# Writing out TensorE's loops over heads and head pairs in a two-layer streaming encoder step

## The chip, the cores and the metric

One Trainium2 chip, one core of it. The time is device microseconds of one execution of the program. Three executions of the kernel before took 3556.9, 3558.29 and 3559.72 us; the median, 3558.29 us, is the time before.

## The reference, cut to what matters

Two consecutive encoder layers are evaluated in one step for a prompt of 1024 frames and a sample of 32 frames, all in float32. Model width is 1024.

```python
# layer 0: x += W_out[ concat( A * silu(zA), B * silu(zB) ) ]
#   A: gated delta rule, 8 heads of 128, causal conv of width 4 on q, k, v,
#      blocks of 64 frames with a triangular solve, state (8, 128, 128)
#   B: chunk-band softmax attention, 16 heads of 64, own chunk and the 8 before it,
#      QK-RMSNorm, learned bias by clipped distance
# layer 1: x += W_out[ GLA * silu(z) ], gated linear attention, 8 heads,
#      dk = 128, dv = 256, gate from a rank-16 projection, state (8, 128, 256)
# after each layer: x += 4-head cross-attention into 256 memory tokens, gated
...
def gdn_block(S, q, k, v, g, beta):
    ...
    sol = lax.linalg.triangular_solve(a_mat, rhs, left_side=True, lower=True)
    u = sol[..., :A_DV] - jnp.einsum('bhjd,bhdv->bhjv', sol[..., A_DV:], S)
    qk = jnp.einsum('bihd,bjhd->bhij', q, k) * dec
    o = (jnp.einsum('bihd,bhdv->bhiv', q, S) * jnp.exp(G)[..., None]
         + jnp.einsum('bhij,bhjv->bhiv', qk, u))
...
def _softmax_attend(q, k, v, bias, valid):
    s = jnp.einsum('bqhd,bkhd->bhqk', q, k).astype(jnp.float32) * (q.shape[-1] ** -0.5)
    ...
    p = jax.nn.softmax(s, axis=-1).astype(v.dtype)
    return jnp.einsum('bhqk,bkhd->bqhd', p, v)
...
def gla_block(S, q, k, v, lg):
    ...
    o = (jnp.einsum('bihd,bhdv->bihv', q * jnp.exp(cb), S)
         + jnp.einsum('bhij,bhjv->bihv', att, v))
```

## The kernel before, in words

The kernel is a row of stages, each a block of five hand-written instruction streams (TensorE, ScalarE, VectorE, GpSimd and the DMA-issuing SyncE) that meet only in counting semaphores; a barrier of all engines stands between two stages (line 45). The stages are: `turn_input` (transposes the input), `gdn` (the delta rule, with the input projection of its heads), `band` (band attention), `finish_layer` for layer 0, `gla` (linear attention) and `finish_layer` for layer 1.

Within `gdn`, `band` and `gla` the work goes head by head. `gdn` and `gla` have 8 heads each; `band` has 8 pairs of heads, since a pair of heads of 64 fills the 128 partitions. On TensorE a head's or a pair's own small matmuls are interleaved by hand with the large projection matmuls of the next one: `fill(n)` lets n steps of the generator `project`, `stream`, `mem_steps` or `early_steps` through, so the order of TensorE's instructions is fixed when the program is built. In `band` the generator `stream(n + 1, 1 - p)` gives the next pair's projection (lines 1462, 1470, 1477 to 1485, 1492), while `scores(u)` (lines 1520 to 1526), `turn(u)` (line 1536) and `values(u)` (line 1556) belong to the pair at hand. `gdn` projects at line 510, `gla` at lines 2020 and 2024.

The first head and the last are written out, since their waits or their filling differ. The heads between them are a loop that the engine's own sequencer runs:

```python
with pe.Fori(1, H_A - 1) as h:      # gdn, line 720: 6 passes, one head each
    head(h, True, True)
...
with pe.Fori(0, 3) as i:            # band, line 1580: 3 passes, two pairs each
    pair(i * 2 + 1, 1, True)
    pair(i * 2 + 2, 0, True)
...
with pe.Fori(1, H_C - 1) as h:      # gla, line 2135: 6 passes, one head each
    head(h, True)
```

In `band` a pass holds two pairs because buffers alternate by the parity of the pair. Tile addresses in a pass are constants; what depends on the pass is the value that each wait compares a semaphore with, such as `h * 6 + 2`, which is computed in registers. A loop's end is a compare and a branch back to its first instruction. The other engines have loops of their own over the same heads (lines 451, 911, 1117 and 1234 in `gdn`, 1427, 1680, 1803 and 1825 in `band`, 1977, 2236, 2348 and 2386 in `gla`).

At the start of a pair in `band`, SyncE issues the load of the next pair's fourth weight tile (line 1366), the stores of the pair's values (lines 1398 and 1399), the store of the attention output (line 1407) and the load of cached values (line 1372). ScalarE copies projections out of PSUM, computes the gate (line 1630, between two loads of activation tables) and the exponentials (line 1648); VectorE adds bias and takes the maximum (lines 1723 and 1726) and normalises (line 1744).

Of the kernel before, what the change touches and what calls it, by code (L numbers as in the profile page):

```python
# [201 lines left out]
H_A = 8  # L202
# [14 lines left out]
def gdn(nc, ident, ones, eps, hT, W, w_ld, w_in, conv_w, conv_state, a_log, dt_bias, onorm_g, state_in,  # L217
# [4 lines left out]
    with ExitStack() as ctx:  # L222
# [65 lines left out]
        mT = [[BT, VV], [KR, KE]]  # L288

        w_mkv = [w.rearrange("(k p) n -> p k n", p=128) for w, _, _, _ in mem_layers]  # L290
        W_mem = [W[:, 2 * x:2 * x + 2, :, :].rearrange("p j k n -> p (j k n)").rearrange("p (k n) -> p k n", k=4) for x in (1, 0)]
        mem_tiles = [[tap[:, 0:1024], U[:, 2, 0:1024]], [zraw[:, 0:1024], sall[:, :, :].rearrange("p h n -> p (h n)")[:, 0:1024]]]
# [77 lines left out]
        with nc.Block() as block:  # L370
# [129 lines left out]
            def _(pe):  # L500
# [216 lines left out]
                pe.wait_ge(padded, 1)  # L717
                pe.wait_ge(o_padded, 1)
                head(0, True, False)
                with pe.Fori(1, H_A - 1) as h:  # L720
                    head(h, True, True)
                head(H_A - 1, False, True)
                turn_out(H_A - 1, 2)
# [534 lines left out]
def band(nc, ident, ones, eps, hT, W, w_ld, w_in, q_g, k_g, rel_bias, cache_k, cache_v, bias_rows,  # L1258
# [6 lines left out]
    with ExitStack() as ctx:  # L1265
# [96 lines left out]
        with nc.Block() as block:  # L1362
# [87 lines left out]
            def _(pe):  # L1450
# [126 lines left out]
                    if m + 1 == ends[place["k", 0]]:  # L1577
                        pe.wait_ge(consts, 2)
                pair(0, 0, True)
                with pe.Fori(0, 3) as i:  # L1580
                    pair(i * 2 + 1, 1, True)
                    pair(i * 2 + 2, 0, True)
                pair(7, 1, False)
# [247 lines left out]
H_C, DV_C, RANK, TAU = 8, 256, 16, 16.0  # L1831
# [14 lines left out]
def gla(nc, ident, ones, eps, hT, W, w_ld, w_in, w_up, gate_bias, onorm_g, state_in, o_dram, state_p, state_s,  # L1846
# [6 lines left out]
    with ExitStack() as ctx:  # L1853
# [76 lines left out]
        SLOT, FIRST = GLA_SLOT, GLA_FIRST  # L1930
        STRIDE = {"q": 128, "k": 128, "z0": 256, "z1": 256}
        LAST = {kind: max(m for m, (x, _) in enumerate(PLAN) if x == kind) for kind in ("z0", "z1", "v", "q", "k")}
        LAST0 = {kind: max(m for m, (x, _) in enumerate(PLAN0) if x == kind) for kind in ("z0", "v", "z1", "q", "k")}


# [23 lines left out]
        with nc.Block() as block:  # L1959
# [46 lines left out]
            def _(pe):  # L2006
# [125 lines left out]
                    if i + 1 == KD * Z0_END:  # L2132
                        turn_lr()
                head(0, True)
                with pe.Fori(1, H_C - 1) as h:
                    head(h, True)
                head(H_C - 1, False)

# [1063 lines left out]
```

## Time and profile before

| what | value |
|---|---|
| median of three executions | 3558.29 us (3556.9 to 3559.72) |
| the profiled execution's own time | 3559.13 us |
| its span, first to last instruction | 3557.4 us |
| TensorE busy in the span | 3482.5 us (98%) |
| VectorE, ScalarE, GpSimd busy | 1173.9, 1102.7, 512.3 us |
| mean granted TensorE clock | 0.994 |
| instruction pages fetched by DMA | q8: 99 packets, 1.62 MB; q14: 62 packets, 0.51 MB |

The profile takes one execution; its span lies 1.7 us under that execution's own time, and that time 0.84 us over the median. PE is TensorE's matmul side and PEld its weight loads, which overlap it; PEldq is TensorE's sequencer, likewise DVEq and ACTq for VectorE and ScalarE. A TensorE wait whose releaser reads "issue" is time in which the engine waited for no semaphore that the profile shows.

### The profile page before, as it was taken

How to read it: one execution, taken by the hardware profiler on the slowest of the kernel's cores; microseconds unless marked ns; L12 is line 12 of the kernel's file. 1: busy time of each engine (PE TensorE's matmuls, PEld its weight loads, DVE VectorE, ACT ScalarE, POOL GpSimd, SP SyncE). 2: the span in 40 equal slices, each digit the busy share in tenths (PEclk: the TensorE clock that was granted, in tenths of full speed). 3: DMA queues.
4: the chain of work that ended last, by engine and by line, in shares of the span. 5: the costliest groups of instructions: out<-in, count | busy, mean ns of one | idle time of the engine just before them, and what ended most of it. 6: DMA issues, size and time to landing. Idle time of an engine off the chain costs nothing. (4 is left out here: it accounts for less than half of the span.)

```text
span 3557.4 us, 47128 instructions
## 1 busy us (share of the span) xinstructions
PE 3482.5 (98%) x16559; PEld 2563.8 (72%) x16559; DVE 1173.9 (33%) x2941; ACT 1102.7 (31%) x2810; POOL 512.3 (14%) x518
## 2 busy tenths in 40 slices
PE   8999999999999989999999998999999999999999
PEld 5777777776577778787766675677777777666676
DVE  2555555555233323333310233022221122220223
ACT  4334333333243433434210342122223122210242
POOL 2445434453000000000000002000000000010000
PEclk9999999999999999999999999999999999999999
DMA  6212411113421332212260102111111111371101
GB/s 160 55 33 38 38 32 31 25 37 109 93 35 35 46 41 45 42 28 87 93 215 30 36 24 74 36 30 43 42 50 40 28 45 39 120 231 48 36 1 49
DMA packets 245487, 206.09 MB, mean 58 GB/s; under 512 B 19903, under 2 KB 222431, under 8 KB 245319
## 3 DMA queue, kind: packets, MB, share of 16 engines
q1 hardware_dynamic: 239966, 194.29, 22.4%
q10 hardware_dynamic: 5360, 9.67, 0.7%
q8 instruction: 99, 1.62, 0.2%
q14 instruction: 62, 0.51, 0.0%
HBM read 157.95 MB, written 45.99 MB: 57 GB/s over the span
## 5 line engine op out<-in xcount | busy, mean ns | idle before, releaser
L510 PE MATMUL gdn_pj<-hT,Wb 128*128 128x352 f32 x1536 | 515.0, 461 | 1.6 <-PEq L45 1.6
L2024 PE MATMUL gla_pj<-hT,Wb 128*128 128x352 f32 x1536 | 473.3, 462 | 6.9 <-PEq L45 6.3
L2024 PEld LDWEIGHTS gla_pj<-hT,Wb 128*128 128x128 f32 x1536 | 291.6, 191 | 157.9 <-issue 10.4
L1462 PE MATMUL band_pj<-hT,Wb 128*128 128x384 f32 (+1 forms) x1152 | 387.2, 465 | 13.9 <-issue 9.0
L510 PEld LDWEIGHTS gdn_pj<-hT,Wb 128*128 128x128 f32 x1536 | 265.7, 191 | 90.0 <-issue 2.9
L1462 PEld LDWEIGHTS band_pj<-hT,Wb 128*128 128x128 f32 x1152 | 207.1, 192 | 97.1 <-issue 16.7
L2020 PE MATMUL gla_pj<-gla_Wv,hT 128*128 128x256 f32 (+1 forms) x1152 | 266.8, 381 | 0.0
L2020 PEld LDWEIGHTS gla_pj<-gla_Wv,hT 128*128 128x128 f32 x1152 | 217.2, 190 | 31.8
L1648 ACT ACTIVATE band_E<-band_NS,band_nm 128x576 f32<-128x576 f32 (+9 forms) x136 | 89.8, 660 | 213.8 <-DVE band_nm L1726 213.6
L1216 POOL TENSOR_TENSOR x_kept<-gdn_AT,gdn_level 128x384 f32<-128x384 f32 x144 | 144.2, 1032 | 35.7 <-DVE gdn_TT L998 18.5
L1492 PE MATMUL band_pj<-Wb,hT 128*128 128x128 f32 x1152 | 144.2, 275 | 0.0
L1556 PEld LDWEIGHTS band_PX<-band_ET,band_VT 128*128 128x128 f32 x976 | 127.0, 192 | 20.3
L1492 PEld LDWEIGHTS band_pj<-Wb,hT 128*128 128x128 f32 x1152 | 136.5, 192 | 0.7
L1726 DVE CUSTOM_DVE_ANT_0 band_NS<-band_SC,band_bias 128x576 f32<-128x576 f32 (+9 forms) x136 | 83.1, 611 | 150.7 <-issue 149.9
L1556 PE MATMUL band_PX<-band_ET,band_VT 128*128 128x128 f32 x976 | 131.0, 275 | 0.0
L2744 PE MATMUL fin_ps<-fin_R,fin_Wx 128*128 128x384 f32 (+1 forms) x384 | 124.7, 468 | 2.2 <-DVE fin_xT L3035 2.1
L2735 PE MATMUL fin_ps<-hT,Wb 128*128 128x384 f32 (+1 forms) x384 | 125.9, 463 | 0.0
L1526 PE MATMUL band_SC<-band_KN,band_Qz 128*128 128x288 f32 (+3 forms) x448 | 115.3, 374 | 3.3 <-issue 3.3
L1658 ACT ACTIVATE band_ET<-band_PT 128x512 f32<-128x512 f32 (+3 forms) x136 | 70.7, 520 | 149.9 <-PE band_PX L1536 89.7
L2708 PE MATMUL fin_ps<-hT,fin_Wq 128*128 128x384 f32 (+1 forms) x384 | 117.2, 459 | 0.0
L2676 PE MATMUL fin_ps<-hT,Wb 128*128 128x384 f32 (+1 forms) x384 | 115.9, 459 | 0.0
L3103 POOL TENSOR_TENSOR fin_acc<-fin_acc,fin_sq 128x384 f32<-128x384 f32 (+1 forms) x42 | 39.0, 929 | 528.3 <-ACT fin_sq L2852 528.2
(417 smaller groups left out, 5364.4 us busy)
## 6 DMA issues: line engine op xcount, KB each, us to landing
Wb<-in_l_w_in_dram SPq DMA_DIRECT2D x96, 512.0 KB, 6.5
fin_xT<-x_features SPq DMA_DIRECT2D x16, 528.0 KB, 8.8
fin_R<-o_features SPq DMA_DIRECT2D x16, 528.0 KB, 9.4
Wb<-in_l_w_mkv_dram SPq DMA_DIRECT2D x8, 1024.0 KB, 5.4
Wb<-in_l_w_out_dram SPq DMA_DIRECT2D x16, 512.0 KB, 3.8
gla_Wv<-in_l_w_in_dram SPq DMA_DIRECT2D x8, 1024.0 KB, 5.3
o_features<-gla_OF ACTq DMA_DIRECT2D x14, 528.0 KB, 5.7
gdn_GB<-gate_rows SPq DMA_DIRECT2D x8, 544.0 KB, 3.6
```

The lines of the kernel that those rows point to most:

```text
L510: mm = pe.matmul(pj[:, m % 2, 0:w], W[:, j, k, :], hT[:, k, c0:c0 + w], start=k == 0, stop=k == KD - 1)
L1216: pool.tensor_tensor(g3(BT, g), g3(AT, g), mask, ALU.mult).then_inc(masked, 1)
L1462: mm = pe.matmul(out[:, 0:w], W[:, BAND_SLOT[j], k, :], hT[:, k, c0:c0 + w], start=k == 0, stop=k == KD - 1)
L1492: mm = pe.matmul(out[:, 0:128], hT[:, k, 128 * i:128 * i + 128], W[:, BAND_SLOT[3], k, :], start=k == 0, stop=k == KD - 1)
L1526: mm = pe.matmul(out[:, b, 0:w], q, KN[p][:, k0 + w * b:k0 + w * b + w], start=True, stop=True)
L1556: mm = pe.matmul(PX[:, 1, :], v, ET[:, u % 2, 128 * b:128 * b + 128], start=b == 0, stop=b == blocks(u) - 1)
L2020: mm = pe.matmul(pj[:, m % 2, 0:wv], hT[:, k, 128 * x:128 * x + 128], Wv[:, k, 0:wv], start=k == 0, stop=k == KD - 1)
L2024: mm = pe.matmul(pj[:, m % 2, 0:w], W[:, SLOT[kind], k, :], hT[:, k, c0:c0 + w], start=k == 0, stop=k == KD - 1)
L2676: mm = pe.matmul(ps[:, 3 * (n % 2) + c, 0:w], weights, src[:, c0:c0 + w], start=i == 0, stop=i == len(tiles) - 1)
L2708: mm = pe.matmul(ps[:, i % 3, 0:w], Wqt[:, h, k, :], hT[:, k, c0:c0 + w], start=k == 0, stop=k == KD - 1)
L2735: mm = pe.matmul(out[:, 0:w], Wz[:, x, k, :], hT[:, k, c0:c0 + w], start=k == 0, stop=k == KD - 1)
L2744: mm = pe.matmul(out[:, 0:w], Wo[:, k, 128 * x:128 * x + 128], O[:, k, c0:c0 + w], start=k == 0, stop=k == M_H - 1)
```

## The change

The three loops over heads or pairs on TensorE become Python loops, so that every pass stands in the instruction stream by itself and the waits of the middle heads compare with constants. The loops of the other engines stay as they are. No matmul, no wait and no buffer is added, removed or moved.

```diff
@@ gdn, tensor engine
                 head(0, True, False)
-                with pe.Fori(1, H_A - 1) as h:
+                for h in range(1, H_A - 1):
                     head(h, True, True)
                 head(H_A - 1, False, True)
@@ band, tensor engine
                 pair(0, 0, True)
-                with pe.Fori(0, 3) as i:
+                for i in range(0, 3):
                     pair(i * 2 + 1, 1, True)
                     pair(i * 2 + 2, 0, True)
                 pair(7, 1, False)
@@ gla, tensor engine
                 head(0, True)
-                with pe.Fori(1, H_C - 1) as h:
+                for h in range(1, H_C - 1):
                     head(h, True)
                 head(H_C - 1, False)
```

## Rows read from the trace of the kernel before

**Rows 1.** The page, busy time of each engine; then TensorE's waits, two rows.
```profile
PE 3482.5 (98%) x16559; PEld 2563.8 (72%) x16559; DVE 1173.9 (33%) x2941; ACT 1102.7 (31%) x2810; POOL 512.3 (14%) x518
...
PE band_pj L1462 <- issue: 9.0, 2, 7.2
...
PE band_SC L1526 <- issue: 3.3, 2, 1.8
```
**Rows 2.** Branches at the loops' ends by line: duration ns min/median/max, first and last start.
```profile
L720 PEldq COMPARE_BRANCH  x6: 76/208/238, 303.4 to 805.3; - x6
...
L1580 PEldq COMPARE_BRANCH  x3: 83/3307/3553, 1287.5 to 1700.9; - x3
...
L2135 PEldq COMPARE_BRANCH  x6: 76/208/234, 2517.3 to 3059.1; - x6
```
**Rows 3.** TensorE's timeline around the band's returns at 1287.5 and 1498.1 us.
```profile
1291.34 0.43 PE L1526 MATMUL band_SC<-band_KN,band_Qz 128*128 128x64 f32 x2 [1.78 <-issue]
...
1303.54 2.29 PE L1462 MATMUL band_pj<-hT,Wb 128*128 128x384 f32 x3 [7.18 <-issue]
...
1501.69 0.43 PE L1526 MATMUL band_SC<-band_KN,band_Qz 128*128 128x64 f32 x2 [1.53 <-issue]
...
1508.54 1.24 PE L1462 MATMUL band_pj<-hT,Wb 128*128 128x384 f32 x3 [1.77 <-issue]
```
**Rows 4.** Band pairs between equal matmuls (L1520): window, length, busy us, PEclk, DMA share, GB/s.
```profile
1171.70:1271.58 99.88, 98.48 (x568) 78.49 (x567) 36.86 (x143) 40.10 (x93) 1.15 (x1) 1.00 0.38 35
1271.58:1382.30 110.72, 101.03 (x568) 79.89 (x567) 36.76 (x143) 40.37 (x93) 1.15 (x1) 0.97 0.26 44
...
1482.18:1585.05 102.87, 98.85 (x568) 78.70 (x567) 36.77 (x143) 40.26 (x93) 1.15 (x1) 1.00 0.20 41
```
**Rows 5.** Windows after the first return, and long DMA bursts elsewhere, same columns.
```profile
1291.30:1301.30 10.00, 5.01 (x18) 2.97 (x18) 1.56 (x11) 3.46 (x7) 0.00 (x0) 1.00 1.02 86
1301.30:1308.10 6.80, 4.56 (x8) 2.83 (x9) 0.84 (x5) 1.42 (x4) 0.00 (x0) 0.50 0.33 112
...
1604.00:1621.00 17.00, 16.32 (x67) 11.03 (x66) 5.15 (x27) 8.39 (x21) 0.00 (x0) 1.00 1.03 334
1800.00:1831.00 31.00, 31.00 (x100) 19.52 (x99) 5.24 (x11) 4.33 (x10) 2.70 (x3) 0.95 1.06 364
```
**Rows 6.** Heads of gdn (two), then of gla (two), between equal matmuls; same columns.
```profile
122.69:223.05 100.36, 99.79 (x568) 77.20 (x567) 56.44 (x133) 38.72 (x132) 45.81 (x43) 1.00 0.18 34
...
423.78:524.15 100.37, 99.88 (x568) 77.27 (x567) 57.10 (x134) 38.67 (x131) 46.33 (x44) 1.00 0.18 33
...
2338.99:2447.35 108.36, 108.36 (x459) 81.39 (x458) 22.30 (x36) 29.67 (x67) 8.01 (x7) 1.00 0.14 42
2447.35:2555.70 108.35, 108.35 (x458) 81.39 (x457) 22.39 (x36) 29.61 (x67) 8.01 (x7) 1.00 0.14 42
```
**Rows 7.** DMA queues in 303.4 to 805.3 us: all packets, then by queue.
```profile
DMA packets 22516, 16.68 MB, mean 33 GB/s; under 512 B 1434, under 2 KB 20724, under 8 KB 22516
...
q1 hardware_dynamic: 22516, 16.68, 21.2%
```
**Rows 8.** Queue q8: whole page; 200 to 303.4; 2408.9 to 2517.3; 1087.6 to 1287.5 us.
```profile
q8 instruction: 99, 1.62, 0.2%
...
q8 instruction: 5, 0.08, 0.3%
...
q8 instruction: 4, 0.07, 0.2%
...
q8 instruction: 10, 0.16, 0.4%
```
**Rows 9.** VectorE's sequencer at the first return, 1286 to 1296 us: branch, next record.
```profile
L1803 DVEq COMPARE_BRANCH  x1: 72/72/72, 1287.4 to 1287.4; - x1
L1803 DVEq FUSED_REGOPS  x1: 99/99/99, 1290.3 to 1290.3; - x1
```
**Rows 10.** Timelines at an undisturbed pair's start: TensorE, VectorE, ScalarE (two).
```profile
1189.51 0.33 PE L1526 MATMUL band_SC<-band_KN,band_Qz 128*128 128x64 f32 x2
...
1190.07 0.06 DVE L1723 MEMSET band_tick<- 128x1 f32 x1 [2.20 <-PE band_SC L1526]
...
1193.70 0.35 ACT L1648 ACTIVATE band_E<-band_NS,band_nm 128x64 f32<-128x64 f32 x1
...
1196.42 0.49 ACT L1596 ACTIVATE band_raw<-band_pj 128x384 f32<-128x384 f32 x1 [1.10 <-PE band_pj L1462]
```

## The prediction

> **What bounds the kernel now.** I read the page first: TensorE is busy 3482.5 of 3557.4 us [rows 1], so only what makes TensorE idle or slow can pay, and 75 us is all the idle time there is. Next the list of waits, for TensorE alone: the largest entry, 9.0 us in two pieces, is "issue" ahead of the band's projection at line 1462, and 3.3 us more in two pieces stands ahead of its scores at line 1526 [rows 1]. "Issue" names no other engine, so the instruction stream itself is suspect. The reader is to look next at the branches that end the three loops on TensorE [rows 2]. In the delta rule and in linear attention a branch takes 208 ns (median of 6); in the band the three take 3.553, 3.307 and 0.083 us, and the last one is the exit. So two returns of the band's loop cost sequencer time, at 1287.5 and 1498.1 us. The timeline shows both: TensorE stands still 1.78 and then 7.18 us after the first, 1.53 and then 1.77 us after the second, no semaphore being late [rows 3]. These four are the "issue" waits of the list.
>
> Why the band alone? Queue q8 moves packets of 16 KB (1.62 MB in 99 packets) [rows 8]; I take them for TensorE's instructions. Between 303.4 and 805.3 us, five whole passes of the delta rule's loop, every packet on the DMA engines belongs to q1 [rows 7]: nothing is fetched, the body is kept. A head there takes about 5 packets the first time, one of linear attention about 4, but the band's pass of two pairs takes 10 and goes on fetching in later passes [rows 8]. My reading is that a body of 5 packets fits in TensorE's instruction memory and one of 10 does not, so the jump back finds its target gone.
>
> **The change part by part.** *Band, line 1580.* The price is best read as pitch, which holds idle time, clock and catching up together. Between equal matmuls a pair that has no return in it takes 99.88 us; the one across the first return 110.72, the one across the second 102.87 [rows 4]. That is 10.84 + 2.99 = 13.83 us. The parts nearly give it too. First return: 1.78 + 7.18 us idle, then 6.8 us at a granted clock of 0.50, the lower of the two levels, right after the long standstill [rows 5]. 4.56 us of matmuls ran in that stretch and would take half at the upper level, 2.28 us. This makes 11.2, less some 0.7 us that TensorE waits for VectorE there in other pairs and did not here (98.48 us busy of 99.88 leaves 1.4 us of ordinary waits a pair [rows 4]). Written out, nothing jumps, and the pair should run like its neighbours. I take 13.83 us.
>
> Does a body that is fetched in a straight line cost anything? The pair at 1171.70 sits in the pass that used 10 packets, and it is one of those at 99.88 us [rows 4, 8]. So no.
>
> *Delta rule, line 720, and linear attention, line 2135.* What goes is 5 taken branches each, 208 ns on the sequencer [rows 2]. The head at 122.69 us is the written-out one, with constants in its waits and no branch; it takes 100.36 us against 100.37 us of a pass in the loop [rows 6]. For linear attention the pair is 108.36 against 108.35 us [rows 6]. So branch, register arithmetic and constants are worth 0.01 us a head at most, 0.1 us over ten returns, and I put nothing in the sum: TensorE's own queue of matmuls covers it. If that cover went, 10 x 0.208 = 2.1 us would be the price; this is the upper bound of the gain here. One rule says otherwise. The Trainium skill, "Advanced Engine Details and Errata", section Control Flow Timing, gives a compare-and-branch about 108 ns; counted on the path ten times this would be 1.1 us more gain. Rows 6 do not bear it out.
>
> What comes is instruction traffic. Five more heads at 5 packets and five at 4 are 45 more, less two or three that the returns in the band fetched anew: q8 should show about 99 + 43 = 142, somewhat fewer since register operations go too. 45 packets of 16 KB are 0.7 MB beside 206 MB, and q8 takes 0.2% of the engines [rows 8]: nothing as bandwidth. As waiting, the lower bound is 0 (the heads that fetch in rows 6 take the pitch of those that don't), the upper bound for one packet is the 7.18 us standstill of rows 3.
>
> *Other queues.* SP's, ScalarE's, VectorE's and GpSimd's instructions are untouched and move past nothing; they run on what TensorE gives them, so all after the returns comes earlier by the same amount. Sum: 3559.13 - 13.83 = 3545.3 us for the profiled execution, which stands 0.84 us over the median; 3558.29 - 13.83 = 3544.46, so 3544.5 us.
>
> **The rivals.**
>
> *1. A new wait takes the place (gain 7 to 12 us).* VectorE and ScalarE keep their loops. At the first return VectorE's branch is at 1287.4 us and its next record at 1290.3 [rows 9], so it seems to miss its target too, under cover of TensorE's standstill. In an undisturbed pair VectorE follows the first scores by 0.56 us (1190.07 after 1189.51) [rows 10]; with scores at 1189.51 + 99.88 = 1289.39 us it would be wanted at 1289.95 and be 0.35 us late. That is covered, since ScalarE's first exponential comes 4.19 us after the scores, behind its table loads [rows 10]. What isn't seen is the other engines' next piece of code. TensorE's own came only after a burst in which the DMA engines were full (share 1.02 from 1291.3 to 1301.3 us) [rows 5]. If ScalarE's did too, its copy of the first projection, due 6.91 us after the scores [rows 10], would be at about 1301.5 instead of 1296.3, some 5 us late, of which the second PSUM bank, one projection job that TensorE may run ahead, covers a part. Price 0 to 5 us; the middle, 2.5 us, gives 3547 us. Against it: after the second return all engines were going again at once when TensorE was, and the pitch there is only 2.99 us over.
>
> *2. The long standstill is not the jump's (gain about 5 us).* The 7.18 and 1.77 us pieces come some 5 us after the jump is over. If they were due to the burst of stores alone, a straight stream would hit them too. Then 8.95 us stay: 3558.3 - 13.83 + 8.95 = 3553.4 us, a change of 0.14%. Against it: each pair starts with the same stores, and no other pair has the gap [rows 4].
>
> *3. Straight fetching stalls in the new heads (slower).* Place: the ten middle heads that now fetch while DMA bursts run. Price: up to 7.18 us a stall [rows 3]. Two stalls of that size eat the gain, three make 3558.3 - 13.83 + 21.5 = 3566 us. It decides once a packet is held back longer than the code before it lasts: 100.37 / 5 = 20 us in the delta rule, 27 us in linear attention. Against it: in bursts of 17 us at 1604 and of 31 us at 1800, with fetching code, TensorE was busy 16.32 of 17 and 31.00 of 31 us [rows 5].
>
> *4. Nothing happens.* If the standstills came from something that merely coincides with the returns, the time stays at 3558. The branch of 3.5 us speaks against it [rows 2]; I leave it 2 in 100, within rival 2's side.
>
> *5. All ten other returns miss too (far faster).* If each return of the other two loops also had to fetch its target, and TensorE paid the branch as it stands in the band, writing them out would give back 10 x 3.3 = 33 us more: about 3511 us. But no packet of q8 runs in five passes of the delta rule's loop [rows 7], and the branch there is 0.208 us [rows 2]; I give it no chance. The Trainium skill, "Runtime: NRT & Kernel Launch", section Instruction fetch mechanics, has this rule: a taken branch whose target lies outside the current two-page window must fetch its page before going on. By that rule bodies of 5 and of 4 packets would miss as well; the trace agrees for the band alone.
>
> **How the numbers follow.** A measurement of this kernel can tell about 0.2%, 7 us, from no change; faster means under 3551.2, slower over 3565.4. Forecast (gain 12.5 to 16 us, 3542 to 3546): 0.73. Rival 1: 0.13. Rivals 2 and 4: 0.08. Rival 3 in full: 0.04; a single stall of it leaves 3551.6 us and counts as no change, 0.02. Rival 5: 0. Faster 0.73 + 0.13 = 0.86, same 0.08 + 0.02 = 0.10, slower 0.04. The range takes in forecast and rival 1: upper end 3550. Lower end 3541: the 2.1 us of branches, and about 1.5 us by which the executions scatter round the median.
>
> **What the profile of the changed kernel would show.** Right: no compare-and-branch on TensorE; no "issue" wait at lines 1462 and 1526; seven equal pitches of 99.88 us in the band, and no stretch at 0.50 clock near 1300 us; heads still at 100.37 and 108.35 us; q8 at 135 to 145 packets with none of them late; a span near 3543.6 us. Rival 1 would show a wait of TensorE for ScalarE (lines 1596 to 1603) or VectorE (line 1744) of over 1 us near 1295 us. Rival 2 would show "issue" at line 1462 without a branch. Rival 3 would show "issue" waits before 920 or after 2400 us. Any of these of 3 us or more in sum makes the sum wrong; a pitch of the middle heads that falls by over 0.1 us would say that I priced the registers' arithmetic too low.

## The result, and the profile after

The kernel after takes 3570.81 us (median of 6 runs, 3568.5 to 3571.53), the one before beside it 3556.99 us (6 runs, 3554.69 to 3559.72): ratio 1.0031, interval 1.002 to 1.0042. It is slower by 0.3%, or 13.8 us. Its profiled execution took 3571.53 us, with a span of 3569.8 us against 3557.4.

Every step foretold for the band is there. First the windows of two pairs of the kernel after, the second of which is the pair that took 110.72 us before [rows 4] (columns: window, its length, busy time of the five engines, granted clock, DMA share, GB/s), then the instruction queues on its page:

```profile
1194.55:1294.42 99.87, 98.47 (x568) 78.48 (x567) 36.87 (x143) 40.12 (x93) 1.15 (x1) 1.00 0.28 41
1294.42:1394.30 99.88, 98.48 (x568) 78.49 (x567) 36.87 (x143) 40.16 (x93) 1.15 (x1) 1.00 0.22 42
```
```profile
q8 instruction: 135, 2.21, 0.2%
q14 instruction: 62, 0.51, 0.0%
```

All seven pitches are 99.88 us, the clock is 1.00, and TensorE's code takes 135 packets where 99 stood [rows 8]. The "issue" waits of [rows 1] are gone from the list. Something else heads it:

```profile
engine line waited for: us in total, times, longest us
PE band_pj L1462 <- PEq L45: 13.6, 1, 13.6
PE gdn_pj L510 <- ACT gdn_zraw L747: 7.7, 1, 7.7
PE gla_pj L2024 <- PEq L45: 6.3, 1, 6.3
```

"PEq L45" is the barrier between two stages: line 45 is where TensorE's sequencer leaves it. Where the 12.4 us of span were lost can be read off marks that exist in both traces: the first transposes of each head of the delta rule (line 566), the first scores of each pair (line 1526), the first matmul of each head at line 2047. The entries are my subtractions of start times.

| stretch between marks | before, us | after, us | difference |
|---|---|---|---|
| start to the first head's mark | 113.95 | 125.91 | +11.96 |
| from there to the first pair's scores (delta rule, barrier) | 875.81 | 886.69 | +10.88 |
| first to last pair of the band | 712.98 | 699.15 | -13.83 |
| to linear attention's first mark | 606.98 | 606.88 | -0.10 |
| its eight heads | 754.55 | 754.91 | +0.36 |
| to the end | 493.13 | 496.26 | +3.13 |

So the band gave exactly what was forecast, and 22.84 us were lost before it, in two places: the start, where nothing that the diff touches has run yet, and the barrier ahead of the band, whose waits the diff leaves alone.

The last row is not the change's. A second execution of the kernel before took 496.2 us for the same stretch, and one of the kernel after 492.7. The difference is granted clock; the kernel before in its first and its second profile (window, length, TensorE's busy time, granted clock, DMA share, GB/s):

```profile
3064.32:3557.36 493.04, 480.96 (x1871) 0.99 0.26 84
```
```profile
3062.90:3559.10 496.20, 484.09 (x1871) 0.98 0.25 84
```

**The start.** First the windows from 24 to 60 us, before and then after (columns as above):

```profile
24.00:60.00 36.00, 33.84 (x140) 17.35 (x138) 4.02 (x8) 5.67 (x13) 7.94 (x30) 0.95 0.84 211
```
```profile
24.00:60.00 36.00, 24.89 (x71) 13.68 (x70) 3.23 (x7) 4.07 (x9) 7.97 (x30) 0.76 0.87 137
```

TensorE is busy 24.9 instead of 33.8 us, the clock is 0.76 instead of 0.95 (up to 120 us it stands at the lower level for 17.1 us in the kernel after and 3.4 before), and the DMA engines are as busy as before (0.87) but move 137 instead of 211 GB/s. In the two timelines (start, duration, engine, line, operation, and in brackets the idle time before it with its releaser) the reader can follow what that does, ScalarE and SyncE's queue before:

```profile
36.02 0.20 ACT L866 ACTIVATE gdn_alog<-gdn_alog 8x1 f32<-8x1 f32 x1 [6.52 <-DMA gdn_onorm<-in_l_a_onorm_g_dram]
...
28.70 3.83 SPq L421 DMA_DIRECT2D gdn_wab<-in_l_w_in_dram  x2
32.58 0.52 SPq L422 DMA_DIRECT2D gdn_alog<-in_l_a_log_dram  x1
```

and TensorE, ScalarE and SyncE's queue after:

```profile
28.71 12.13 PE L510 MATMUL gdn_pj<-hT,Wb 128*128 128x352 f32 x32 [2.84 <-PEq L45]
48.54 7.74 PE L510 MATMUL gdn_pj<-hT,Wb 128*128 128x352 f32 x16 [7.70 <-ACT gdn_zraw L747]
...
47.94 0.20 ACT L866 ACTIVATE gdn_alog<-gdn_alog 8x1 f32<-8x1 f32 x1 [17.99 <-DMA gdn_onorm<-in_l_a_onorm_g_dram]
48.05 0.78 ACT L747 ACTIVATE gdn_zraw<-gdn_pj 128x352 f32<-128x352 f32 x2
...
29.16 10.52 SPq L421 DMA_DIRECT2D gdn_wab<-in_l_w_in_dram  x2
39.73 4.90 SPq L422 DMA_DIRECT2D gdn_alog<-in_l_a_log_dram  x1
```

TensorE fills its two PSUM banks and waits 7.70 us for ScalarE to copy the first. ScalarE is still waiting for three tiny parameters (lines 422 to 424), whose loads SyncE issues behind the weight loads. The line on the last three of the first head's four weight tiles, before and after, and the DMA engines while they run:

```profile
DMA to landing us min/median/max: 17.0/20.9/20.9
```
```profile
DMA to landing us min/median/max: 26.6/27.5/29.5
```
```profile
14.00:34.00 20.00, 16.16 (x107) 12.89 (x106) 14.02 (x19) 12.79 (x26) 5.38 (x21) 0.91 0.97 109
```
```profile
14.00:34.00 20.00, 15.22 (x99) 12.12 (x99) 13.23 (x18) 12.43 (x26) 4.92 (x20) 0.83 0.98 69
```

These are the same loads of the same 512 KB tiles, issued within 1.3 us of the same time. They have only become slower: the engines count as full in both kernels (0.97, 0.98), and move 109 GB/s in one and 69 in the other.

**The barrier ahead of the band** is the same loss again. The band's first loads are issued by the delta rule's SyncE in advance (line 59), again tiles of layer 0's input weight. SyncE's queue before, then after, and the waits of SyncE and TensorE, before and then after:

```profile
916.13 0.99 SPq L480 DMA_DIRECT2D out_dram<-gdn_U  x2
917.16 1.20 SPq L59 DMA_DIRECT2D Wb<-in_l_w_in_dram  x2
```
```profile
927.96 4.02 SPq L480 DMA_DIRECT2D out_dram<-gdn_U  x2
932.02 3.33 SPq L59 DMA_DIRECT2D Wb<-in_l_w_in_dram  x2
```
```profile
SPq L497 <- DMA out_dram<-gdn_U: 1.0, 1, 1.0
PE band_pj L1462 <- PEq L45: 1.9, 1, 1.9
```
```profile
SPq L497 <- DMA out_dram<-gdn_U: 7.9, 1, 7.9
PE band_pj L1462 <- PEq L45: 13.6, 1, 13.6
```

The last stores of the stage run beside the slow weight loads and land 14.8 us after their issue. SyncE waits for them before it enters the barrier, and TensorE stands 13.6 us there; from 900 to 1000 us the clock is at its lower level for 17.1 us, where it was 6.8 before.

**One series made the loads of all later runs comparable:** the mean time from issue to landing of the four 512 KB weight tiles of each head of the delta rule (head 0 to 7) and each pair of the band, worked out from the trace's records of these loads, in us.

```
               delta rule, heads 0 to 7                    band, pairs 0 to 7
before         18.5  6.1  6.6  7.7 11.5  8.0  7.1  5.4    11.5  5.4  7.4  8.2 11.8  8.6  7.1  5.8
after          26.0  9.0  8.3  6.3  9.2  5.9  8.4  8.9    20.9  9.2  9.1  6.9  9.1  6.6  8.8  9.7
```

The loads have rows of 512 bytes. Some heads' columns load fast and some slowly, the band's pairs mostly repeat what the delta rule's heads show, and the pattern differs between the two kernels. I call it the series below. The 28 loads of layer 1's input weight at line 1966, equal tiles with equal rows, took 3.8, 3.9 and 5.7 us (shortest, median, longest) before and 3.8, 4.0 and 5.0 after.

### The profile page after: what moved, and what is told of

Same layout as the page of the kernel before. It is cut to its first block and busy times, and to the rows that moved or that the text cites. A ratio compares the mean times of both kernels' runs of the same rounds, so it can differ in the third digit from the quotient of the medians.

```text
span 3569.8 us, 46360 instructions
## 1 busy us (share of the span) xinstructions
PE 3485.4 (98%) x16559; PEld 2564.5 (72%) x16559; DVE 1173.7 (33%) x2941; ACT 1103.3 (31%) x2810; POOL 512.7 (14%) x518
## 5 line engine op out<-in xcount | busy, mean ns | idle before, releaser
L2024 PEld LDWEIGHTS gla_pj<-hT,Wb 128*128 128x128 f32 x1536 | 291.6, 191 | 158.3 <-issue 11.5
L1462 PE MATMUL band_pj<-hT,Wb 128*128 128x384 f32 (+1 forms) x1152 | 384.5, 462 | 16.6 <-PEq L45 13.6
L1216 POOL TENSOR_TENSOR x_kept<-gdn_AT,gdn_level 128x384 f32<-128x384 f32 x144 | 144.2, 1032 | 35.6 <-DVE gdn_TT L998 18.4
```

The lines of the kernel that those rows point to most:

```text
L1216: pool.tensor_tensor(g3(BT, g), g3(AT, g), mask, ALU.mult).then_inc(masked, 1)
L1462: mm = pe.matmul(out[:, 0:w], W[:, BAND_SLOT[j], k, :], hT[:, k, c0:c0 + w], start=k == 0, stop=k == KD - 1)
L2024: mm = pe.matmul(pj[:, m % 2, 0:w], W[:, SLOT[kind], k, :], hT[:, k, c0:c0 + w], start=k == 0, stop=k == KD - 1)
```

## The experiments

### Is it repeatable, and which part of the change does it?

Both kernels again (no edit), and two halves of the change, in one sitting on one chip.

> The kernel before, unchanged. Theory 1: load times of the layer-0 weight tiles head by head as in the first profile (5.6 us for head 1, near 12 us for head 4, 8 us for heads 5 to 6, 11.5 us in the band's pair 4), barrier wait 1.9 us, 3555 to 3560 us. Theory 2: another pattern, and a time that may lie 10 us off.

> The changed kernel once more, nothing else. In the first profile of it the band ran at 99.88 us a pair, as forecast, but TensorE stood 7.70 us in the delta rule's first projection (about 40.8 us) and 13.6 us at the barrier before the band (931 us), and the loads of weight tiles of layer 0 took other times than before (first four tiles 20 to 30 us instead of 15 to 21; head 3 8.9 instead of 12 us). Theory 1 (the build decides: how large the program is decides where its tensors lie in device memory, and so how fast 512-byte rows of the layer-0 input weight come): the same pattern of load times head by head, both standstills again within 1 us, 3568 to 3572 us. Theory 2 (each loading of a program draws its own memory): another pattern, the standstills of another size, a time anywhere from 3545 to 3575 us. Theory 3 (TensorE's 36 more code packets crowd the DMA engines): the standstills again, and code packets inside the slow stretches.

> Only the band's loop written out; the loops of the delta rule and of linear attention stay. All theories: seven band pairs at 99.88 us, no branch there, 13.8 us less in the band; q8 at about 97 packets. Theory 3 (code traffic of the new heads crowds the DMA engines): no new traffic, so nothing is lost, 3557.0 - 13.8 = 3543 us. Theory 1: the program is larger by four pairs only; its start and its barrier at 920 us take what the placement gives, so 3543 us if it falls as in the kernel before, up to 3568 us if it falls as in the changed one; the load times of the tiles and the two standstills move together. Theory 2: as theory 1, but not repeatable.

```diff
 # band_only: the kernel after, with two of the loops put back
-                for h in range(1, H_A - 1):      # line 720
+                with pe.Fori(1, H_A - 1) as h:
...
-                for h in range(1, H_C - 1):      # line 2135
+                with pe.Fori(1, H_C - 1) as h:
```

> Only the loops of the delta rule and of linear attention written out; the band keeps its loop and both its standstills (110.7 and 102.9 us across the returns). Theory 3: all of the loss of the changed kernel and none of its gain, 3571 + 13.8 = 3585 us. Theory 1: q8 at about 137; the time is 3557 plus whatever the placement costs, 0 to 25 us, and the load times of the tiles say how much. Heads at 100.37 us either way.

```diff
 # gdn_gla_only: the kernel after, with the band's loop put back
-                for i in range(0, 3):            # line 1580
+                with pe.Fori(0, 3) as i:
```

Measured, with ratios to before: after 3568.47 us (1.0028, interval 1.0017 to 1.004), band alone 3548.22 us (0.9968, 0.9957 to 0.998), delta rule and linear attention alone 3552.38 us (0.9982, 0.9973 to 0.9992); before, one run, 3560.89 us. The series of the two known kernels came back to within 0.5 us a head, and the start, the barrier and the band's pitches with it, so this is a property of the built program and no noise. The halves:

```
band alone     10.9  6.9  6.0  5.8  6.5  9.8 10.0  7.5     6.4  6.6  5.8  6.8  7.3 10.6  9.7  6.8
gdn and gla    15.2  8.9  6.0  9.1  6.2  8.3  8.6 13.8    10.7  8.9  6.2  9.2  6.6  9.0  9.0 14.5
```

Each half alone is faster than before, and together they are slower: no fixed cost of each part can give that. The band's two slow pitches, with its loop left in, were 102.92 and 100.98 us in the second kernel, not 110.72 and 102.87, with 1.1 us more in its last pair: the same return can cost very different times.

Band alone gave 11 us and not 13.83, since its start is 6.05 us later than before's (first mark at 120.00 us). Its first head's four tiles land sooner, in 10.9 us instead of 18.5, so head 0 of the series does not foretell the start. What comes late are small loads of the same weight: the second load at line 421 lands 13.4 us after its issue (6.3 before). TensorE's and ScalarE's rows of band alone:

```profile
PE gdn_pj L510 <- ACT gdn_zraw L747: 3.7, 1, 3.7
```
```profile
42.15 0.20 ACT L866 ACTIVATE gdn_alog<-gdn_alog 8x1 f32<-8x1 f32 x1 [13.20 <-DMA gdn_onorm<-in_l_a_onorm_g_dram]
```

### The scratch, or another engine's code?

Small shifts of the memory layout (16 more rows of the scratch tensor for features, 68 KB), and a loop of another engine written out (GpSimd's in linear attention, about 8 KB; ScalarE's in the delta rule, about 72 KB).

> The kernel before with 16 unused rows (67584 bytes, that is 2048 over a multiple of 4096) added to the scratch tensor of mixer outputs: not one instruction differs. Of a head's four weight tiles the mean landing time was by head 18, 6, 7, 8, 11.5, 8, 7, 5 us in both profiles of the kernel before, and another series in every other program. Placement theory: if scratch tensors push the layer-0 input weight, the slow head moves (half of 4096 bytes would be four heads of 512 bytes, from head 4 to head 0 or 8), and the start and the barrier at 920 us lose up to 20 us, 3557 to 3580 us. If only the code's size counts: the same series and 3555 to 3563 us. Theory 3 (code packets): the same series.

> The changed kernel with the same 16 unused scratch rows. Placement by scratch: the slow head moves from 0 to 4, the start's 7.7 us and the barrier's 13.6 us go to near 0 and 1.9 us, and the time falls to about 3557 - 13.8 = 3543 us. Placement by code alone: 3566 to 3572 us with the same series (26, 9, 8, 6, 9, 6, 8, 9 us). Theory 3: the same, 3566 to 3572 us.

```diff
-    o_dram = scratch("o_features", [2048, NTOK])
+    o_dram = scratch("o_features", [2048 + 16, NTOK])[0:2048, :]
```

> The kernel before with GpSimd's loop in linear attention written out (some 120 instructions more on an engine that is 86% idle); TensorE's stream is the same and q8 stays at 99 packets. Placement theory: another series of load times by head, and with it another start, another barrier wait and another standstill after the band's returns; the time anywhere in 3545 to 3580 us. Theory 3 (TensorE's code packets): the same series, 3555 to 3563 us.

> The changed kernel with GpSimd's loop in linear attention written out as well; TensorE's stream and its 135 code packets stay. Placement theory: another series, so another start and barrier: 3543 us if the slow head is none of head 0, up to 3575 us. Theory 3 (TensorE's code packets make the loss): nothing that matters changes, 3566 to 3572 us. In all cases the band at 99.88 us a pair.

```diff
-                with pool.Fori(1, H_C - 1) as h:     # line 2386
+                for h in range(1, H_C - 1):
```

> The kernel before with ScalarE's loop in the delta rule written out (some 1100 instructions, 72 KB, more than the 8 KB by which GpSimd's loop in linear attention changed nothing); TensorE's stream is that of the kernel before. If any code of that size moves the weights in device memory: another series of load times by head than 18, 6, 7, 8, 11.5, 8, 7, 5 us. If TensorE's code alone does it: the same series and 3555 to 3563 us.

```diff
-                with act.Fori(1, H_A - 1) as h:      # line 911
+                for h in range(1, H_A - 1):
```

Measured: 3560.73 (one run), 3569.93 (1.0028, 1.0015 to 1.004), 3559.22 (one run), 3571.49 (1.003, 1.0014 to 1.0046) and 3555.42 us (one run). All five kept the series of the kernel that they were built from to within 0.8 us a head of the delta rule (ScalarE's: 18.4, 6.4, 6.7, 7.7, 11.5, 8.0, 6.6, 5.4), and its waits at the start and the barrier to within 0.6 us. I read this as "only TensorE's code counts". That was wrong, as the last runs show: the pieces were too small. The pitch across the second return was 104.6 and 104.9 us in before_scratch and before_pool, where the kernel before had 102.87 and 102.92.

### Is it what stands in line behind the loads?

If the small loads and the last stores only suffer by standing behind the weight loads in SyncE's queue, another queue should free them. band_own has the same edit as after_own, on band_only.

> The changed kernel with two small transfers taken off the queue of the slow loads: the three tiny loads for the delta rule's gates are issued by ScalarE at its start, and the last two stores of memory keys and values too, by ScalarE behind its own copies. The weight loads stay as slow as in the changed kernel (series 26, 9, 8, 6, 9, 6, 8, 9 us). Queue theory (the loss is what waits in line behind the slow loads): ScalarE is free at about 33 instead of 48 us, the 7.7 us standstill becomes 0 to 3 us, the barrier before the band ends near 935 instead of 944 us; 3570 - 5 - 9 - 3 to 6 us of half clock = 3550 to 3556 us. If TensorE itself waited for the slow weight tiles: the standstills move to the tiles and the time stays at 3565 to 3571 us.

> Only the band's loop written out, and the same two transfers on ScalarE's queue. Its 3.7 us standstill at 39 us goes, with some of the half clock behind it; series of load times as in the version with the band alone (11, 7, 6, 6, 6.5, 10, 10, 7.5 us). Queue theory: 3548.2 - 4 to 7 us, so 3541 to 3545 us, faster than both kernels. Otherwise 3547 to 3549 us.

```diff
-                sp.dma_start(alog[:, :], a_log.unsqueeze(1)).then_inc(ld_small, 16)
...
+                act.dma_start(alog[:, :], a_log.unsqueeze(1)).then_inc(ld_small, 16)
...
-                    if x % 2:
+                    if x % 2 and x < 7:
...
+                    if x == 3:
+                        act.wait_ge(mk_out, i + 1)
+                        act.dma_start(mem_layers[1][3][128 * m:128 * m + 128, :], mem_out[m]).then_inc(mk_st[m], 16)
```

Measured: 3572.35 us (1.004, 1.0026 to 1.0054) for the kernel after, 3549.03 us (0.9975, 0.9965 to 0.9985) for band alone; both forecasts of a gain failed. Waits of TensorE and of SyncE in the first, then of TensorE in the second:

```profile
PE band_pj L1465 <- PEq L45: 19.4, 1, 19.4
...
PE gdn_pj L507 <- ACT gdn_zraw L744: 5.1, 1, 5.1
...
SPq L494 <- DMA out_dram<-gdn_U: 16.8, 1, 16.8
```
```profile
PE band_pj L1465 <- PEq L45: 4.8, 1, 4.8
PE gdn_pj L507 <- ACT gdn_zraw L744: 0.7, 1, 0.7
```

The edit has two parts, and the traces tell them apart. The tiny loads gained by it: the first wait fell from 7.7 to 5.1 us and the first mark came 3.95 us sooner, and on band alone the wait fell from 3.7 to 0.7 and the mark came 5.29 us sooner (114.71 us). So standing in line was part of the start's loss. The stores lost it again: the barrier's wait rose from 13.6 to 19.4 us, and from 1.9 to 4.8. In the kernel after they were issued earlier, at 919.35 and 924.61 us instead of 927.96 and 928.59. But SyncE, freed of them, also issued the last two weight loads 8 us earlier (4 us of both come from the start), and the stores landed 19.0 and 21.1 us after their issue instead of 14.8. A run with the tiny loads alone moved was not made.

### Which loop, or how much code?

Linear attention alone leaves all code that runs before 2400 us as it was.

> Only linear attention's loop written out, which runs 1400 us after the last load of the layer-0 input weight. Placement theory: the series of load times in the delta rule and the band changes all the same. Theory 3 (code packets in flight): series and standstills of the kernel before, since no code before 2400 us differs. Either way 108.41 instead of 108.35 us per head of linear attention, as in the two programs that had it written out.

```diff
 # gla_only: the kernel before, with line 2135 written out
-                with pe.Fori(1, H_C - 1) as h:
+                for h in range(1, H_C - 1):
```

> Delta rule and band written out, linear attention back in its loop. TensorE's code is then about as long (some 0.70 MB more than before, counted as trace records of 64 bytes) as in the kernel with delta rule and linear attention written out, but other code. Theory A (the length of TensorE's code alone decides which head's weight loads are slow): mean landing of the four weight tiles by head of the delta rule like that kernel's (15, 9, 6, 9, 6, 8, 9, 14 us; band 11, 9, 6, 9, 7, 9, 9, 15), TensorE's wait for the first head's copy 2 to 4 us, the one at the barrier ahead of the band 2 to 5 us, all seven band pitches 99.88 us, linear attention's heads 108.36 us, so 3552.4 less the 3 + 1.1 + 1.1 us that its band lost, less 0.4 us: about 3547 us. Theory B (which loop is written out decides): the series of the kernel with all three (26, 9, 8, ...), a barrier wait of 13 us, and about 3569 us.

```diff
 # gdn_band: the kernel after, with line 2135 put back in its loop
-                for h in range(1, H_C - 1):
+                with pe.Fori(1, H_C - 1) as h:
```

> Delta rule alone written out (about 0.38 MB more code). Theory A (length decides): the series by head like those of band alone and of linear attention alone (11, 7, 6, 6, 6.5, 9, 10, 7 us), first wait 3 to 4 us, barrier about 2 us, returns of the band's loop still missing (pitches over 102 us twice), about 3560 us within 4. Theory B (the delta rule's own code written out is what slows the loads beside it): first head's tiles 20 us and more, about 3580 us.

```diff
 # gdn_only: the kernel before, with line 720 written out
-                with pe.Fori(1, H_A - 1) as h:
+                for h in range(1, H_A - 1):
```

Measured: 3563.01 (one run), 3553.6 (0.9985, 0.9975 to 0.9995) and 3547.2 us (one run). I order all series by how much code was added. The size is an estimate: the trace's TensorE records times 64 bytes (a written-out head of the delta rule is 1200 records, one of linear attention 953, and two pairs of the band 2362). The last column is the first head's mark.

```
MB added                 delta rule, heads 0 to 7                    first mark
0     before             18.5  6.1  6.6  7.7 11.5  8.0  7.1  5.4    113.95
0.30  band_only          10.9  6.9  6.0  5.8  6.5  9.8 10.0  7.5    120.00
0.31  gla_only           11.6  6.7  6.5  5.7  6.5  8.8 10.8  7.4    120.43
0.38  gdn_only           13.4  7.1  8.0  5.9  8.1  8.4 13.7  8.8    114.44
0.69  gdn_gla_only       15.2  8.9  6.0  9.1  6.2  8.3  8.6 13.8    118.49
0.69  gdn_band           14.4  9.2  5.7  8.9  5.7  8.0  8.5 13.8    118.61
0.99  after              26.0  9.0  8.3  6.3  9.2  5.9  8.4  8.9    125.91
```

gdn_gla_only and gdn_band share only one loop but have the same length and the same series, to 0.8 us. So have gla_only and band_only, which share none (1.0 us). A slow head moves on with the length: head 4, heads 5 and 6, 6, 7, and in the kernel after it has come round to head 0, the one whose loads nothing covers at the start and at the band's barrier. The start's mark does not follow one head, but it too moves with added code that has not run yet: gla_only runs the very instructions of the kernel before up to 2400 us and starts 6.5 us later. The time of gdn_band was forecast too low (3547): it loses 0.9 us in its last pair, and its profile has 496.2 us from line 2047's last mark to the end, where band_only has 491.5. That stretch scatters with the granted clock, also between two executions of one kernel; why its ten executions stay at 3550.83 to 3555.95 us isn't shown.

gdn_only, forecast at about 3560 us, took 3547.2: its returns were nearly free, with pitches of 100.79 and 102.07 us. The series does not explain that, since the tiles that it loaded around the second return were among its slowest (13.3 us in the mean; the one issued at 1491.3 us took 13.6). The waits do, in part:

```profile
PE band_SC L1526 <- issue: 3.3, 2, 1.7
```

The waits at line 1526 stand as before, but those at line 1462 (9.0 us in [rows 1]) are gone. They are gone in gdn_gla_only too, and present in every kernel that keeps both the band's and the delta rule's loop. So whether the standstill at line 1462 occurs goes with what code lies ahead of the band's, and not with the loads alone. No run tests that further.

### Code that never runs

If length decides, code that a branch jumps over must do the same. It was put at the very end of one engine's stream, in the last stage.

> The kernel before with about 1 MB of TensorE code at the very end that a branch jumps over (7856 transposes, two records each): nothing of it ever runs. Theory A (length of the code alone decides the speed of the early weight loads): the series by head changes from 18, 6, 7, 8, 12, 8, 7, 5 us to something like after's (26, 9, 8, 6, 9, 6, 8, 9 us), the wait for the first head's copy goes from 1 to about 8 us and the barrier's from 2 to 8 to 13 us; slower by 5 to 22 us, 3562 to 3580. Theory C (only code that is run matters, or where in the stream the run code lies): series and waits as before, time within 4 us of before's.

> The kernel after with about 0.32 MB of TensorE code at the very end that is jumped over (2496 transposes). Theory A (length decides, and the slow head moves with it by one for some 0.25 MB): the series by head is no longer after's, the slow head is past head 0, first wait 2 to 4 us and barrier 2 to 5 us, time 3545 to 3555 us, so faster than before. Theory C (only code that runs matters): series 26, 9, 8, 6, 9, 6, 8, 9 us, waits 7.7 and 13.3 us, 3569 to 3571 us.

```diff
+                if l == 1:
+                    r = pe.alloc_register()
+                    pe.reg_mov(r, 0)
+                    with pe.If_ne(r, 0):
+                        for _ in range(982):          # after_dead: 312
+                            turn_y(0, range(KD))
```

> The kernel before with 15712 activations at the very end of ScalarE's stream that a branch jumps over (one record each, so again about 1 MB by 64 bytes a record, this time in ScalarE's code). Theory A1 (only the length of TensorE's code counts): series by head as before's (18, 6, 7, 8, 12, 8, 7, 5 us), barrier wait 2 us, time within 4 us of before's. Theory A2 (the length of any engine's code counts, and the 72 KB and 8 KB tried earlier were only too small to see): the series moves as with 1 MB of dead TensorE code (26, 9, 8, 6, 9, 6, 8, 9 us), barrier wait 13 us, first wait 6 to 8 us, about 3576 us.

> The kernel before with 0.32 MB of dead TensorE code (2496 transposes). Theory A (length alone): the series of linear attention alone or band alone written out (11 to 12, 7, 6.5, 6, 6.5, 9, 10, 7 us), so no loss at the start or the barrier; the returns of the band's loop still miss, with losses of 3 to 14 us over the 99.88 us pitches as the loads at those pairs fall; 3555 to 3564 us. Theory D (the dead code works only together with code that runs, as in the kernel after with dead code): series and pitches of before, 110.7 and 102.9 us, time within 3 us of before's.

```diff
+                    with act.If_ne(r, 0):             # ScalarE, in before_deadact
+                        for _ in range(15712):
+                            act.activation(yS[0][0:128, 0:512], ps[0:128, 0, :], ACT.Copy)
```

(before_dead_small is before_dead with 312 in place of 982.)

| kernel | dead code | median us (runs) | ratio to before, interval |
|---|---|---|---|
| before_dead | 1.0 MB, TensorE | 3576.26 (4) | 1.0046, 1.0029 to 1.0062 |
| after_dead | 0.32 MB, TensorE | 3547.9 (5) | 0.9959, 0.9945 to 0.9973 |
| before_dead_small | 0.32 MB, TensorE | 3560.09 (10) | 1.0007, 0.9997 to 1.0016 |
| before_deadact | 1.0 MB, ScalarE | 3550.02 (10) | 0.9975, 0.9965 to 0.9984 |

```
                         delta rule, heads 0 to 7                    first mark
before_dead_small  0.32  11.7  6.3  6.9  5.7  6.6  8.0 11.4  8.0    115.65
before_dead        1.0   25.6  8.9  8.2  6.1  8.9  6.4  8.3  8.6    123.93
after_dead         1.31  13.0 12.2  7.8  7.4  5.3  7.5  5.5  7.1    114.37
before_deadact     1.0   14.4 14.3  9.1  8.9  6.3  8.5  5.7  8.1    113.82
```

The waits of TensorE in before_dead, which runs the loops of the kernel before:

```profile
PE band_pj L1462 <- PEq L45: 13.0, 1, 13.0
PE band_pj L1462 <- issue: 8.9, 2, 5.2
PE gla_pj L2024 <- PEq L45: 6.3, 1, 6.3
PE gdn_pj L510 <- ACT gdn_zraw L747: 5.8, 1, 5.8
```

It has the losses of both kernels at once: the kernel after's series to within 0.5 us a head, its first mark at 123.93 us, its barrier wait of 13.0, and the band's missed returns besides. after_dead runs what the kernel after runs, and both losses are gone; the window from 14 to 34 us of before_dead, and of after_dead:

```profile
14.00:34.00 20.00, 15.58 (x100) 12.31 (x99) 13.60 (x18) 12.32 (x26) 5.23 (x21) 0.84 1.02 75
```
```profile
14.00:34.00 20.00, 16.76 (x104) 12.83 (x103) 13.38 (x18) 12.68 (x26) 5.92 (x23) 0.83 0.65 109
```

At 1.02 of their time the DMA engines moved 75 GB/s, and at 0.65 of it 109. before_dead_small reproduces gla_only (11.6, 6.7, 6.5, 5.7, 6.5, 8.8, 10.8, 7.4) to 0.8 us in the delta rule, and its returns: the pitches are 103.37 and 108.68 us, 12.3 us over, where gla_only's were 103.09 and 109.08. Its start is 4.8 us earlier, so the match is not complete. Beside before (110.72 and 102.87 us, the same code in the same order) it shows that added code elsewhere changes what a return costs. The slow tile moved with the cost (the one issued just after the first return took 12.3 us before and 6.6 here, just before the second 7.4 and 11.9); whether it is the cause isn't shown. before_deadact settles the point that I had wrong: ScalarE's code does it too. Its time was forecast at about 3576 us, with the series of TensorE's 1.0 MB, and neither came. The series is near after_dead's instead, within 2.1 us, as if more code had been added than TensorE's 1.0 MB, so one sum of bytes by my estimate does not order all kernels. Its start is as good as before's (first mark 113.82 us), and its slow pitches shrink to 102.50 and 102.89 us, 5.6 us over in place of 13.83:

```profile
PE band_SC L1526 <- issue: 3.2, 2, 1.7
PE band_pj L1462 <- issue: 3.0, 2, 1.8
```

**What is shown and what isn't.** Shown: added code, run or not, TensorE's or ScalarE's, changes how fast the 512-byte-row loads of one weight matrix go, head by head, and kernels with about the same length of added TensorE code share a series. before and before_dead run the same instructions, and the first pair's scores come at 989.76 us in one and 1010.20 in the other. Adding 0.32 MB of code that never runs made the kernel after some 20 us faster (3547.9 us, 0.9959 of before; without it 3570.81 and 3568.47 us, 1.0031 and 1.0028). Not shown is by what path. A longer program may place the tensors at other addresses in the device memory; no run moved a tensor by itself far enough (68 KB did nothing, 0.30 MB of code did), and no trace has addresses. Nor was the layout of the matrix varied: a row of layer 0's input weight is 8208 numbers or 32,832 bytes, 64 over 32 KB, and one of layer 1's, whose loads never slowed, is 6160 numbers or 24,640 bytes. That stays open.

## Why the prediction was wrong

- **Band, 13.83 us.** Right, to the digit: 712.98 less 699.15 us between the first and last pair's scores, seven pitches of 99.88 us, clock 1.00, no "issue" wait at lines 1462 and 1526. It is the price in this build: the same stretch took 711.44 us with 0.32 MB of dead code, 704.80 with ScalarE's 1.0 MB, and 715.13 with a scratch tensor 68 KB larger.
- **Branches of the other two loops at nothing.** Right. The delta rule's middle heads took 100.35 instead of 100.37 us (703.83 against 703.91 us over seven), so the 2.1 us of the upper bound did not appear. Nor did the 1.1 us by the 108 ns that the Trainium skill, "Advanced Engine Details and Errata", section Control Flow Timing, gives a compare-and-branch. The windows of [rows 6] that were taken for written-out heads end 20 and 38 us inside the loops, which start at 203.0 and 2409.0 us; the reading held even so. Linear attention's heads took 108.41 instead of 108.35 us, 0.36 us over all; that goes with its loop written out, and why isn't shown. gdn_gla_only and gla_only show the same 108.41, and gdn_band, which has that loop back, 108.35.
- **Instruction traffic.** Right as to packets (135, foretold 135 to 145), and fetching in a straight line stalled nothing: the only "issue" wait over the whole list is one of 0.2 us.
- **"SP's, ScalarE's, VectorE's and GpSimd's instructions are untouched and move past nothing ... so all after the returns comes earlier by the same amount."** This is the step that failed. The instructions were untouched, but their transfers were not: since no instruction of theirs had changed, the sum put at nothing what the loads ahead of the band could lose, and their slowing cost +11.96 us at the start and +10.88 us at the barrier, by waits and by the lower clock after them. The +3.13 us of the last stages is scatter between executions: TensorE stands there 13.7 us at the lower clock level instead of 6.8 (leaving out the last 6 us), and the kernel before did so too in its second profile.
- **The range.** It priced stalls of code fetches only. Its lower end allowed for the scatter of the executions, nothing allowed for a program of another length being another draw of load speeds. The same edit with 0.32 MB of dead code gives 3547.9 us, inside 3541 to 3550, with the start and the barrier as before and the band at 99.88 us a pair.
- **The rivals.** Rival 1 (an engine that keeps its loop is late): no; no wait of over 1 us for ScalarE or VectorE near 1295 us. Rival 2 (the long standstill isn't the jump's): no as stated, since no written-out pair has it, but half true: the pair across the first return takes 110.72, 103.37, 103.09, 102.50 or 100.79 us in kernels whose band is the same. Without the jump there is no gap; its length goes with the added code (before_dead_small), and the piece at line 1462 also with the code ahead of the band (gdn_only). Rival 3 gave the sign and, at 3566 us, nearly the time, by a mechanism that did not occur: no "issue" wait stands in the new heads. Rival 4: no, since the pitches changed. Rival 5: none of it, as [rows 7] said. By the two-page rule of the Trainium skill, "Runtime: NRT & Kernel Launch", section Instruction fetch mechanics, the delta rule's and linear attention's loops would have missed at each return. The runs do not agree: writing them out gave back 0.1 us and cost 0.36.

What the profile before could have told: the window from 14 to 34 us has full DMA engines at 109 GB/s where layer 1's equal tiles land in 3.9 us (median), and layer 0's take 5.4 to 18.5 us in the mean of a head. A cost that differs threefold between equal transfers hangs on something that the code does not state, and an edit may move it.

## What to carry to other kernels

When a change alters the length of the code, compare first the landing times of loads that it does not touch, load by load, before and after; if they moved, the change's own worth must be read from pitches inside its stage (here -13.83 us) and not from the total. A control with the same added length in code that never runs helps to separate the two; its match was close here, not complete. If the total matters, write out only the loop that misses its return (band alone: 3548.22 us, 0.9968 of before; it too is one draw of the loads), and look to the loads with short rows that nothing covers, at the start and ahead of a barrier.

## What was unexpected in the hardware

- Equal 512 KB loads with 512-byte rows took from 5.2 to 26.3 us in the mean of a head, repeatably for one build, by head and by the length of the code; the DMA engines count as full (0.97 to 1.02) while they move 69 to 109 GB/s.
- Code that is never run changed a kernel by +16 us (before_dead against its before, 3576.26 to 3560.49), by nothing clear of noise (before_dead_small, 3560.09 to 3558.57) or by -9 us (1 MB on ScalarE, 3550.02 to 3558.57).
- A return of the same loop whose branch took over 3 us cost from 0.9 to 11.2 us in pitch between builds. The standstill at line 1462 vanished in both kernels that had the delta rule's loop written out and the band's not.
